# Moving the first step's weight transfers from the sync engine's queue to ScalarE's in a two-layer encoder

## The reference

```python
def rmsnorm(x, g):
    y = xf * lax.rsqrt(jnp.mean(xf * xf, axis=-1, keepdims=True) + EPS)
    return (y * g.astype(jnp.float32)).astype(x.dtype)

def swiglu(x, wg, wu, wd):
    return (jax.nn.silu(x @ wg) * (x @ wu)) @ wd
...
    for layer in range(DEPTH):
        x = x + 0.5 * swiglu(rmsnorm(x, norm_g[layer, 0]), ffn_w_gate[layer, 0], ...)
        xn = rmsnorm(x, norm_g[layer, 1])
        ...
        x = x + mix
        x = x + 0.5 * swiglu(rmsnorm(x, norm_g[layer, 2]), ffn_w_gate[layer, 1], ...)
```

## Time and profile before

| what | us |
|---|---|
| median of 3 timed runs | 1833.74 (1833.67 to 1834.15) |
| the profiled execution, its own time | 1835.04 |
| span of the profiled execution, first to last instruction | 1833.2 |
| TensorE busy in it | 1823.1 |
| VectorE busy | 1361.2 |
| ScalarE busy | 827.1 |

### The profile page before, as it was taken

One profiled execution on the slowest core, in us unless ns is written; L12 is line 12 of the kernel. 1 busy time (PEld: TensorE's weight loads), 2 busy tenths in 40 slices (PEclk: granted clock), 3 DMA queues, 4 the chain that ended last, 5 costly groups with the idle time before them and its releaser, 6 DMA issues.

```text
span 1833.2 us, 26257 instructions
## 1 busy us (share of the span) xinstructions
PE 1823.1 (99%) x9996; PEld 1562.0 (85%) x9996; DVE 1361.2 (74%) x2120; ACT 827.1 (45%) x1357; POOL 300.1 (16%) x239
## 2 busy tenths in 40 slices
PE   9999999999999999999999999999999999999999
PEld 7888988978888988989889898897777788989889
DVE  7686866978866768768767686687887666858657
ACT  6343443643343433435434343465666543434433
POOL 0310401223102104012031130211111003104011
PEclk9999999999999999999999999999999999999999
DMA  5244235532222322346323223642222232322354
GB/s 189 75 144 121 92 116 153 127 121 72 93 103 86 122 92 92 116 133 166 115 70 115 93 100 107 169 127 88 77 74 86 70 115 75 133 92 92 115 150 126
DMA packets 75420, 201.81 MB, mean 110 GB/s; under 512 B 14665, under 2 KB 27626, under 8 KB 75307
## 3 DMA queue, kind: packets, MB, share of 16 engines
q1 hardware_dynamic: 54784, 178.28, 28.3%
q0 software_dynamic: 6912, 12.59, 3.9%
q10 hardware_dynamic: 13610, 9.41, 1.9%
HBM read 185.57 MB, written 3.93 MB: 103 GB/s over the span
## 4 chain that ended last, share of the span: by engine, by line
PE 92%; DVE 5%; issue 1%; ACT 1%; DMA 0%; SPq 0%; DVEq 0%; ACTq 0%
PE bank L1522 25%; PE bank L1524 25%; PE bank L1523 25%; PE bank L1473 5%; PE bank L1476 4%; PE bank L1477 4%; PE bank L1735 1%; PE bank L1726 1%; DVE t L1063 1%; DVE wlr L487 1%; DVE x L1242 0%; DVE wlr L510 0%; PE bank L1745 0%; PE bank L1715 0%; PE bank L1751 0%
## 5 line engine op out<-in xcount | busy, mean ns | idle before, releaser
L1522 PE MATMUL bank<-xh,whr 128*128 128x512 f32 x1408 | 551.1, 391 | 0.7 <-DVE wlr L487 0.5
L1523 PE MATMUL bank<-xl,whr 128*128 128x512 f32 x1408 | 548.6, 390 | 0.0
L1524 PE MATMUL bank<-xh,wlr 128*128 128x512 f32 x1408 | 548.6, 390 | 0.0
L478 ACT ACTIVATE whr<-rest 128x512 fp32r<-128x512 f32 (+1 forms) x445 | 273.6, 616 | 456.5 <-PE bank L1524 444.6
L487 DVE TENSOR_TENSOR wlr<-rest,whr 128x512 fp32r<-128x512 f32 (+1 forms) x445 | 326.8, 738 | 118.2 <-ACT whr L478 115.7
L1522 PE MATMUL bank<-hsh,whr 128*128 128x256 f32 x1232 | 349.5, 284 | 1.1 <-DVE x L1242 0.9
L1523 PE MATMUL bank<-hsl,whr 128*128 128x256 f32 x1232 | 348.6, 283 | 0.0
L1524 PE MATMUL bank<-hsh,wlr 128*128 128x256 f32 x1232 | 348.6, 283 | 0.0
L1522 PEld LDWEIGHTS bank<-xh,whr 128*128 128x128 f32 x1408 | 264.8, 188 | 58.7 <-issue 2.1
L1523 PEld LDWEIGHTS bank<-xl,whr 128*128 128x128 f32 x1408 | 264.9, 188 | 55.5 <-issue 1.0
L1524 PEld LDWEIGHTS bank<-xh,wlr 128*128 128x128 f32 x1408 | 264.7, 188 | 55.1
(11 more groups left out here) (201 smaller groups left out, 2138.6 us busy)
## 6 DMA issues: line engine op xcount, KB each, us to landing
rest<-in_ffn_w_gate SPq DMA_DIRECT2D x61, 512.0 KB, 3.7
rest<-in_ffn_w_up SPq DMA_DIRECT2D x61, 512.0 KB, 4.6
rest<-in_ffn_w_down SPq DMA_DIRECT2D x54, 512.0 KB, 4.5
raw_area<-in_ffn_w_gate SPq DMA_DIRECT2D x26, 512.0 KB, 3.8
raw_area<-in_ffn_w_up SPq DMA_DIRECT2D x26, 512.0 KB, 4.7
raw_area<-in_ffn_w_down SPq DMA_DIRECT2D x26, 512.0 KB, 4.5
raw_area<-in_w_qkv SPq DMA_DIRECT2D x24, 512.0 KB, 3.5
raw_area<-in_w_in_ab SPq DMA_DIRECT2D x16, 512.0 KB, 3.5
```

Of the source, the lines that this page charges most:

```text
L478: act.activation(whr[:, at:at + st.kb, :].rearrange("p k c -> p (k c)"), weights(st, buf)[:, 0, :], ACT.Copy).then_inc(high, 1)
L1522: pe.matmul(out, whr[:, at, :], hi, start=start, stop=False, skip_group_check=onto)
L1523: pe.matmul(out, whr[:, at, :], lo, start=False, stop=False, skip_group_check=onto)
L1524: return pe.matmul(out, wlr[:, at, :], hi, start=False, stop=stop, skip_group_check=onto)
```

## The change

The four halves of the first step are asked for by ScalarE's program instead of SyncE's: the two first halves right behind the parameters, the two second halves after block 1 has been put in ScalarE's queue, ahead of chunk 1. SyncE asks for the six pieces of x one behind the other and then for the second step.

```diff
@@ SyncE: run(ph)
                     if ph.before is None and st.t == 0:
-                        bring_x(0)
-                        bring_first_weights(st, 0, 0)
-                        bring_first_weights(st, 1, 0)
-                        for n in range(1, 4):
+                        for n in range(len(X_PIECES)):
                             bring_x(n)
-                        bring_first_weights(st, 0, 1)
-                        for n in range(4, 6):
-                            bring_x(n)
-                        bring_first_weights(st, 1, 1)
                         continue
@@ ScalarE
+            def bring_first_weights(st, which, half):
+                size = KD // 2 * P
+                act.dma_start(weights(st, B_A11 + 2 * which + half)[:, 0, :],
+                             (wu if which else wg)[0, 0, :, half * size:(half + 1) * size])\
+                  .then_inc(step_in[st.set][which] if half else first_in[which], 16)
+
             act.dma_start(vec[:, :], a["v_params"]).then_inc(vec_in, 16)
+            for which in range(2):
+                bring_first_weights(phases[0].steps[0], which, 0)
@@ ScalarE: for d in range(KD)
                 if d == 0:
                     block_high(act, phases[0], 0)
                     block_high(act, phases[0], 1)
+                    for which in range(2):
+                        bring_first_weights(phases[0].steps[0], which, 1)
```

More of the change, by code:

```diff
@@ L364, in bring_x @@
                              a["x_tokens"][:, at.start * TOK:at.stop * TOK]).then_inc(x_in[n], 16)
[L366 to L370, removed]
             def bring_weights(ph, i, j):
```

## The result

The changed kernel takes 1837.20 us in the median of 17 executions (1836.65 to 1838.60), the kernel before 1833.75 (17 executions, 1832.68 to 1835.89): ratio 1.0021, 95% interval 1.0014 to 1.0027. That is 3.45 us slower, and 1.2 us above the top of the forecast range (1836.0). The profiled execution took 1837.09 for a span of 1835.3.

A forecast was written before the change was run, and what follows sets the result against it. The prediction took the opening as held up by arrivals, then TensorE running without pause from 9.44. Its terms, -0.07 + 0.25 = +0.2 us, gave a forecast median of 1833.9 us, range 1833.1 to 1836.0.

The forecast's parts named there:

- The step on the first halves: Opening: gate and up halves share the engines with x's pieces, landing at 5.2 and 6.5; first matmul at 6.75.
- The term of -0.07 us: First halves' share of the sum: second chunk starts at 9.31 instead of 9.44, 0.07 us gained at the upper clock.
- lands after 7.5: Sign of being wrong: the up half landing after 7.5, with a pause inside the first chunk.
- the bound of 8.5: Upper bound for the up half's landing, behind all x pieces beside it: second chunk at 11.2, 0.9 us lost.
- a rival with 7 in 100: TensorE's clock rises later after a late up half: at most 2.8 us lost, half likelier; 7 in 100.
- The bound on T: Third block: wg's second half may land (T) up to 12.4 at no cost; past that each us costs one.
- The latency: wg's second half on ACT's queue: asked for at 6.6, 5.6 plus 0.4 us to land, at 12.6.
- the 0.25 of the sum: Second halves' term: wg's second half lands at 12.6 against a limit of 12.35, costing 0.25 us.
- nothing behind 25 us: From about 25 us the matmuls are the chain; a difference over 1 us in sum there would show it wrong.
- chunk 2 was in time: Second chunk of x lands by about 6.5, is ready by 9.0 (9.4); TensorE does not wait for it.
- ACT's queue did not starve: Rival: second halves wait until the sync queue drains, landing at 18.3, costing 5.9 us (1839.6); 4 in 100.
- 3.67 us: 0.2% of this kernel, about what a measurement can tell from no change; 95 in 100 for staying within it.

The follow-up runs named there:

- the second profile of before: The kernel before, unchanged, run once more for another profile: 1833.19 us, span 1831.4.
- Held x: The changed kernel, with SyncE asking for x's second piece only when the parameters have landed: 1835.75 us, ratio 1.0011.
- the run with the first halves alone: The changed kernel with the two second halves back in SyncE's queue, first halves staying on ACT's queue: 1836.08 us, ratio 1.0012.
- the pair with 9 and 14 warm-ups: First halves on ACT's queue, second halves back with SyncE, with 9 warm-up matmuls (1836.08 us) and with 14 (1834.26 us).
- the first experiment: The changed kernel with the two first halves back in SyncE's queue, second halves staying on ACT's queue: 1836.39 us, ratio 1.0015.
- the early one: First halves with SyncE, second halves on ACT's queue but asked for behind the rounding of chunk 0: 1835.14 us, ratio 1.0009.

## Why the prediction was wrong

**Where the 3.45 us are.** Between the second profile of before and the one after, the up block starts at 9.44 for 7.26 and the second chunk at 10.88 for 8.73, 2.15 late; the 18 matmuls from there to the third block take 6.03 for 4.21, another 1.82 at the lower clock. Together 3.97, which the matmul on the sums shows (27.11 for 23.14) and the span keeps (1835.3 for 1831.4, 3.9). The 2.05 us between the profiled execution of before and the one after hide this, as the former had its own late rise and a later x. (The second profile is 0.56 us under the median of before, so 3.97 is somewhat more than the 3.45 of the medians.)

**The step on the first halves failed.** I let each half share with one piece of x and put gate at 5.2 and up at 6.5, inside bounds of 5.83 and 8.5 for up; they were 6.1 and 8.0. Held x gives 5.2 for up, so the sharing was the right mechanism and its size wrong: by 8.0 the sync queue had moved as much as four pieces of x beside the two halves, not two. The term of -0.07 us in the sum became 2.26 us in the run with the first halves alone, the clock included. I had named "lands after 7.5" as what would show me wrong, but priced the bound of 8.5 at 0.9 us; that was worked out against a profile with a late clock and a late x, and against the second one the second chunk is 2.15 late.

**The clock was put with the wrong case.** It stood as a rival with 7 in 100 because I forecast no longer pauses than before. With the halves at 6.1 and 8.0 there were pauses of 2.14 and 0.81, and the clock cost 1.8 us in the profile and 1.5 in the pair with 9 and 14 warm-ups. The price was inside the rival's 1.4 to 2.8, but the mechanism was not quite the rival's: the clock did not rise later. It was up for the first block (its matmuls at 7.86 and 8.09 are 0.23 apart) and fell right behind it, after the pause that the late gate half had lengthened.

**The bound on T was taken from one execution.** T up to 12.4 came from a third block at 14.40, with the clock up at 11.1. In the second profile of before the eighth chunk is needed at 14.98 instead of 16.45, so by the same working T may be 10.9 at most. The latency was right (6.0 forecast, 5.9 measured). In the first experiment, with the second halves alone, T was 12.2, which by this bound costs 1.3 us and not the 0.25 of the sum; that profile shows 1.59 at the sums and 2.0 in the span, the medians 2.57. The working left out the second wait, near 38 us. In the changed kernel T comes to 13.97, since the up half that it is asked for behind came late, and it is covered only because TensorE is late as well; once the clock was kept up, the wait for it showed (1.56 us).

**What held.** In the changed kernel nothing behind 25 us adds to the loss (3.97 at the sums, 3.9 in the span); chunk 2 was in time. ACT's queue did not starve until the sync queue was empty. The loss of 3.45 is under 3.67 us by the medians, but the interval, 2.6 to 5.0 us, leaves that open.

## What to carry to other kernels

Here a second queue added no bandwidth (415 GB/s from 8.2 to 14.9; 413 and 424 in like stretches of before), it changed who is first: keep off it what the first instruction waits for. A margin read from one profile is only as good as the clock and the arrivals in it, so take a second profile of the same kernel before pricing a move against a cover of 2 us. A pause of 2 us on TensorE costs more than itself when the clock falls behind it, and two edits that use up the same slack don't add.

## What the runs showed of the hardware

With the sync queue loaded, ACT's queue ran no packet for 3 to 4 us behind an issue: 3.4 us in the changed kernel, 3.85 in the early one, while the other queue moved 1.1 to 1.4 MB. Then both took turns. DMA packets of the changed kernel from 8.0 to 11.4, then from 11.6 to 15.0:

```profile
q1 hardware_dynamic: 395, 1.43, 103.2%
...
q1 hardware_dynamic: 252, 0.92, 66.2%
q10 hardware_dynamic: 256, 0.49, 37.3%
```

There are 252 packets against 256, but mostly of 4 KB against 2 KB (0.92 MB against 0.49), so ACT's queue gets a third of the bytes. The Trainium skill ("DMA: Bandwidth & Descriptors", section "Queues, rings and completion order") has each engine take turns between queues by packets; the second stretch agrees, the first shows a wait ahead of it that the rule alone would not give. Part of it is there with little queued: from 0.75, where the changed kernel asks for the parameters as its first transfer on ACT's queue, to 2.35 only SyncE's packets ran.

```profile
q1 hardware_dynamic: 33, 0.07, 31.4%
```

By that, an estimate, about 1.6 us are the issue's own and some 2 us more are the wait. What sets it stays open: holding the later steps' weights did not shorten it (3.7 us in all), and with x held no packet ran for 1.8 us in one profile, hardly more than with nothing queued.

The moment at which TensorE's clock rises differed between executions of one kernel: 11.1 in the first profile of before, ahead of 8.73 in the second.
